# A three-layer block on one core: products with the high weights and products with the low weights, grouped by eight or taken in turns

## Chip, core and metric

The kernel runs on one core of one Trainium2 chip. The metric is the device time of one execution in microseconds. TensorE multiplies, ScalarE and VectorE evacuate, cast and subtract, SyncE issues the loads of the weights.

## What is computed

The input `x` is 256 tokens by 1024 features in float32. It goes through two mixer layers with an MLP each, and then through a layer with attention and a short convolution side by side:

```python
def first_block(x, ...):
    for l in range(2):
        h = rmsnorm(x, g[0])
        y = even_mixer(h, ...) if l % 2 == 0 else odd_mixer(h, ...)
        x = x + rmsnorm(y, g[1])
        h = rmsnorm(x, g[2])
        x = x + rmsnorm(sq_relu_mlp(h, mlp_w1[l], mlp_w2[l]), g[3])
    return x

def sq_relu_mlp(h, w1, w2):            # w1: 1024 x 4096, w2: 4096 x 1024
    return jnp.square(jax.nn.relu(h @ w1)) @ w2

def hybrid_layer(x, c, ...):
    h = rmsnorm_2(x, norm_g) * (1 + scale[:, None, :]) + shift[:, None, :]
    proj = h @ w_in                     # 1024 x 10240
    q, k, v, g_attn, cb, cc, cx, g_conv, m_attn, m_conv = jnp.split(proj, IN_OFFSETS, axis=-1)
    ...
    return x + gate[:, None, :] * (merged @ w_out)
```

The change concerns two kinds of these products: `h @ w1` of both MLPs, and the columns q, k, g_attn, cc, cx, cb and g_conv of `h @ w_in`.

## The kernel before

The weights come in units of 1 MB (a list `UNITS`, taken in order through a ring of buffers `raw`). Each unit is split into a high part `wh` (float32r, a cast on ScalarE) and a low part `wl` (the remainder, a subtraction on VectorE). The activation `h` is split likewise; for each slab `k` of 128 features, `hx[:, k, :, :]` holds the high part `hh` and the low part `hl` side by side, 256 tokens each. A product of float32 accuracy is high by high, plus high weights by low activation, plus low weights by high activation.

A feature-major unit ("F") holds 1024 input features by 256 output features. The 128 x 128 weights are the stationary operand, and the tokens stream. For most of these units both activation parts stream behind one load of the high weights: 512 columns into a whole bank of PSUM, `hh` into its first half and `hl` into its second. The low weights then take `hh` alone, 256 columns, and add to the bank's first half. The evacuation adds the two halves. In what follows a *wide* product is one of the 512-column ones with the high weights, a *narrow* product one of the 256-column ones with the low weights.

`both_parts(o, u, g)` issues this for one half `g` (128 output features) of a unit: 8 wide and 8 narrow products, one of each for every slab. It is called from `f_up` (roles `up0` and `up1`, 14 units each, the first two of the 16 up-projection units of a layer being token-major) and from `f_wide` (roles `aq`, `ak`, `ag`, `cc`, `cx`, `cb`, `cg`, 4 units each). The first `aq` unit is in `LOW_LAST`: it has a loop of its own, with all its wide products first, and isn't changed. The order of the work on TensorE is that of the loop over the units in the program. All waits of a group, for `hi`, `lo` and the bank, stand before its first product; the signal (`used`, `up_half`) goes with its last.

Down-projection units ("B") stream 512 weight columns behind `yh` or `yl`, in the order high, low, high; token-major units ("T") stream 512 weight columns behind `hh` or `hl`. Every product goes through one helper, `mm`, on line 672, so the trace has one line for all of them and they are told apart by their tiles. In the trace `hx,wh` is an F product with the high weights, `hx,wl` one with the low weights, `wh,hx` and `wl,hx` are T products, `yh` and `yl` stand for B products. LDWEIGHTS is the load of the stationary operand, on a row of its own, PEld.

Of the kernel before, what the change touches and what calls it, by code (L numbers as in the profile page):

```python
# [27 lines left out]
KT = D // P  # L28
# [240 lines left out]
def build(nc, a, out):  # L269
    ctx = ExitStack()  # L270
    with ctx:
# [284 lines left out]
        def slot(t, u):  # L556
            return part(t, u).rearrange("p (k c) -> p k c", k=SLABS[UNITS[u][0]])
# [112 lines left out]
        def _(eng):  # L670
            def mm(o, l, r, start, stop):
                return eng.matmul(o, l, r, start=start, stop=stop, skip_group_check=True)  # L672
# [65 lines left out]
            def both_parts(o, u, g):  # L738

                c = slice(g * P, (g + 1) * P)  # L740
                for k in range(KT):
                    mm(o[:, :], slot(wh, u)[:, k, c], hx[:, k, :, :].rearrange("p a t -> p (a t)"), k == 0, False)
                for k in range(KT):
                    m = mm(o[:, 0:SEQ], slot(wl, u)[:, k, c], hh[:, k, :], False, k == KT - 1)
                return m

            def f_up(u):
                layer, i = UPS.index(UNITS[u][4]), UNITS[u][5]
                for g in range(2):
                    n, o = up_block(u, g)  # L750
                    first = 2 * (i - 2) + g
                    if first < 2:
                        wait_evac(eng, at(UNITS[u][4].replace("up", "uw"), 1), first)
                    elif first == 2:
                        eng.wait_ge(S["x_row"], 2 * layer + 1)
                    else:
                        eng.wait_ge(S["up_sum"], n - 2)
                    both_parts(o, u, g).then_inc(S["used" if g else "up_half"], 1)

            def f_wide(u):  # L760

                n, w_hi, w_lo = WIDE_OF[u], slot(wh, u), slot(wl, u)
                if PAIR_OF[u] == (0, 1):
                    for t in range(TT):
                        wait_bank(eng, u, t)
                else:
                    for v in [v for v in WIDE_OF if v < u and PAIR_OF[v] == PAIR_OF[u]][-1:]:
                        wait_evac(eng, v)
                if u not in LOW_LAST:
                    for g in range(2):  # L770
                        m = both_parts(wide_bank(u, g), u, g)
                else:
                    for g in range(2):
                        for k in range(KT):
                            mm(wide_bank(u, g)[:, :], w_hi[:, k, g * P:(g + 1) * P], hx[:, k, :, :].rearrange("p a t -> p (a t)"), k == 0, False)
                    wait_low(eng, u)
                    for g in range(2):
                        for k in range(KT):
                            m = mm(wide_bank(u, g)[:, 0:SEQ], w_lo[:, k, g * P:(g + 1) * P], hh[:, k, :], False, k == KT - 1)
                m.then_inc(S["used"], 1)  # L780
# [1511 lines left out]
```

## Time and profile before

| | before |
|---|---|
| median of 3 runs | 974.04 us (973.6 to 974.58) |
| span of the profiled execution | 972.0 us |
| TensorE products busy | 964.2 us, 99%, 5192 of them |
| VectorE, ScalarE busy | 682.1 us (70%), 539.9 us (56%) |
| chain that ended last | TensorE 96%, line 672 alone 94% |
| granted TensorE clock | 0.999 of full speed over the span |

The profile gives no time of its own for the profiled execution beside its span; the span is 2.0 us below the median of the runs. A start in the timeline has a resolution of 0.01 us. The busy time of a row of products includes the latency of the last one, so paces are read from the starts and not from it.

### The profile page before, as it was taken

What the parts mean: (1) busy time and instruction counts of PE and PEld (TensorE: products, weight loads), DVE (VectorE), ACT (ScalarE), POOL (GpSimd) and SP (SyncE); (2) the same over time, 40 slices, a digit from 0 to 9 for tenths busy, and PEclk for the clock granted to TensorE, in tenths of its full rate; (3) what the DMA queues carried; (4) which work ended last, traced back from release to release, by engine and by line L of the source; (5) the groups of instructions that cost most, each with busy time, mean ns of one, the idle gap of its engine ahead of it and who ended that gap; (6) DMA issues with size and microseconds to landing.
All of it is one profiled execution on the core that took longest, in us unless ns stands there. A gap on an engine that the chain in (4) does not pass through costs nothing.

```text
span 972.0 us, 13041 instructions
## 1 busy us (share of the span) xinstructions
PE 964.2 (99%) x5192; PEld 832.9 (86%) x5192; DVE 682.1 (70%) x917; ACT 539.9 (56%) x733; POOL 13.9 (1%) x12
## 2 busy tenths in 40 slices
PE   9999999999999999999999999999999999999997
PEld 8898888888888888988888888887888888888886
DVE  6989646687677767866687767768554888756474
ACT  7844464664555457655674455558445576545533
POOL 0000000000000000000000000000000000002000
PEclk9999999999999999999999999999999999999999
DMA  9954526467776674534467777773855544566611
GB/s 330 302 174 130 173 89 197 130 228 265 226 242 225 231 245 135 178 130 130 152 216 256 242 225 243 247 219 117 271 194 178 170 139 165 173 215 221 207 51 43
DMA packets 122863, 187.27 MB, mean 193 GB/s; under 512 B 5331, under 2 KB 88756, under 8 KB 122804
## 3 DMA queue, kind: packets, MB, share of 16 engines
q1 hardware_dynamic: 122368, 186.05, 58.1%
q8 instruction: 41, 0.67, 0.3%
q10 hardware_dynamic: 436, 0.40, 0.1%
q14 instruction: 18, 0.15, 0.0%
HBM read 185.37 MB, written 1.06 MB: 192 GB/s over the span
## 4 chain that ended last, share of the span: by engine, by line
PE 96%; DVE 3%; ACT 1%; issue 0%; ACTq 0%
PE bank L672 94%; DVE arena L1236 1%; DVE wl L1230 1%; PE bank L936 1%; PE bank L1026 0%; ACT arena L1843 0%; DVE arena L1233 0%; DVE arena L1230 0%; PE bank L1109 0%; ACT L1843 0%; ACT wh L1848 0%; PE bank L879 0%; PE bank L735 0%; PE bank L945 0%; ACT sd L1843 0%
## 5 line engine op out<-in xcount | busy, mean ns | idle before, releaser
L1230 DVE TENSOR_TENSOR wl<-raw,wh 128x2048 fp32r<-128x2048 f32 (+1 forms) x157 | 356.7, 2275 | 152.1 <-ACT wh L1848 128.1
L1848 ACT CAST wh<-raw 128x2048 fp32r<-128x2048 f32 x155 | 294.7, 1911 | 142.7 <-PE bank L672 141.0
L672 PE MATMUL bank<-hx,wh 128*128 128x512 f32 (+1 forms) x1280 | 296.6, 364 | 0.1
L672 PEld LDWEIGHTS bank<-hx,wh 128*128 128x128 f32 x1280 | 219.4, 190 | 30.4 <-issue 0.7
L672 PE MATMUL bank<-wh,hx 128*128 128x512 f32 x576 | 184.5, 394 | 0.8 <-ACT hx L1843 0.5
L672 PE MATMUL bank<-hx,wl 128*128 128x256 f32 x1088 | 174.3, 282 | 0.0
L672 PEld LDWEIGHTS bank<-hx,wl 128*128 128x128 f32 x1088 | 156.7, 190 | 8.9
L672 PE MATMUL bank<-wh,yh 128*128 128x512 f32 (+1 forms) x420 | 163.4, 389 | 0.0
L672 PE MATMUL bank<-wl,yh 128*128 128x512 f32 (+1 forms) x420 | 162.7, 387 | 0.0
L672 PE MATMUL bank<-wh,yl 128*128 128x512 f32 (+1 forms) x420 | 162.6, 387 | 0.0
L672 PEld LDWEIGHTS bank<-wh,hx 128*128 128x128 f32 x576 | 107.8, 188 | 24.3 <-issue 2.0
L672 PE MATMUL bank<-wl,hx 128*128 128x512 f32 x288 | 112.2, 390 | 0.0
L672 PEld LDWEIGHTS bank<-wh,yl 128*128 128x128 f32 x420 | 78.9, 188 | 16.2
L672 PEld LDWEIGHTS bank<-wh,yh 128*128 128x128 f32 x420 | 78.9, 188 | 15.5
L672 PEld LDWEIGHTS bank<-wl,yh 128*128 128x128 f32 x420 | 79.0, 188 | 15.3
L1230 DVE TENSOR_TENSOR arena<-bank,arena 128x256 f32<-128x256 f32 (+1 forms) x89 | 40.7, 488 | 44.3 <-ACT arena L2195 29.5
L672 PEld LDWEIGHTS bank<-wl,hx 128*128 128x128 f32 x288 | 54.1, 188 | 10.6
L2195 ACT COPY arena<-bank 128x256 f32<-128x256 f32 x56 | 18.1, 376 | 74.1 <-PE bank L672 74.1
L1988 ACT COPY work<-bank 128x256 f32<-128x256 f32 x56 | 20.6, 368 | 52.2 <-PE bank L672 52.2
L1843 ACT ACTIVATE arena<-bank 128x512 f32<-128x512 f32 (+2 forms) x58 | 28.4, 498 | 32.9 <-PE bank L672 32.8
L1236 DVE SCALAR_TENSOR_TENSOR arena<-raw,cf,arena 128x256 f32<-128x256 f32 x84 | 40.7, 485 | 3.0
L1843 ACT ACT_TABLE_LOAD x26 | 33.4, 1283 | 4.3 <-PE bank L672 2.0
(187 smaller groups left out, 675.0 us busy)
## 6 DMA issues: line engine op xcount, KB each, us to landing
raw<-in_mlp_w SPq DMA_DIRECT2D x64, 1024.0 KB, 5.4
raw<-in_w_in SPq DMA_DIRECT2D x40, 1024.0 KB, 5.1
raw<-in_ev_w_in SPq DMA_DIRECT2D x19, 1024.0 KB, 5.5
raw<-in_w_ada SPq DMA_DIRECT2D x12, 1024.0 KB, 5.1
raw<-in_od_w_in SPq DMA_DIRECT2D x12, 1024.0 KB, 5.2
raw<-in_ev_w_out SPq DMA_DIRECT2D x6, 1024.0 KB, 4.9
raw<-in_od_w_out SPq DMA_DIRECT2D x4, 1024.0 KB, 4.8
raw<-in_w_o_conv SPq DMA_DIRECT2D x4, 1024.0 KB, 4.8
```

Source lines behind the costliest of these rows:

```text
L672: return eng.matmul(o, l, r, start=start, stop=stop, skip_group_check=True)
L936: m = eng.transpose(x_half(t, k), src[:, t, k * P:(k + 1) * P], ident[:, :])
L1230: return eng.tensor_tensor(o, x, y, op)
L1236: return eng.scalar_tensor_tensor(out=o, in0=x, scalar=c, in1=y, op0=op0, op1=op1)
L1843: return eng.activation(o, x, f, **more)
L1848: eng.copy(part(wh, u), part(raw, u)).then_inc(S["hi"], 1)
L1988: eng.copy(up_home(i)[:, g * SEQ:(g + 1) * SEQ], up_block(u, g)[1][:, SEQ:2 * SEQ]).then_inc(S["up_low"], 1)
L2195: m = eng.copy(wide_home(u, g), wide_bank(u, g)[:, SEQ:2 * SEQ])
```

## The change

The second loop header is taken out of `both_parts`. Before, the eight wide products of a half run one after another and then the eight narrow ones; after, each wide product is followed by the narrow one of the same slab. The products, their operands, the banks, the waits and the signals are the same.

```diff
             def both_parts(o, u, g):
 
                 c = slice(g * P, (g + 1) * P)
                 for k in range(KT):
                     mm(o[:, :], slot(wh, u)[:, k, c], hx[:, k, :, :].rearrange("p a t -> p (a t)"), k == 0, False)
-                for k in range(KT):
                     m = mm(o[:, 0:SEQ], slot(wl, u)[:, k, c], hh[:, k, :], False, k == KT - 1)
                 return m
```

TensorE's instruction order before, where the first `up0` unit follows on the token-major units of the same layer (the last columns name the bank that is written and the two operands; x8 is eight in a row):

```order
L672 MATMUL bank1<-wh_50,hx_53 128x512 x8
L672 MATMUL bank3<-ident_67,rs_77 128x128 x2
L672 MATMUL bank0<-hx_53,wh_50 128x512 x8
L672 MATMUL bank0<-hx_53,wl_51 128x256 x8
L672 MATMUL bank1<-hx_53,wh_50 128x512 x8
L672 MATMUL bank1<-hx_53,wl_51 128x256 x8
```

The same place after:

```order
L672 MATMUL bank1<-wh_50,hx_53 128x512 x8
L672 MATMUL bank3<-ident_67,rs_77 128x128 x2
L672 MATMUL bank0<-hx_53,wh_50 128x512
L672 MATMUL bank0<-hx_53,wl_51 128x256
L672 MATMUL bank0<-hx_53,wh_50 128x512
L672 MATMUL bank0<-hx_53,wl_51 128x256
```

The two rows of eight have become eight pairs; the rows ahead of them are where they were.

The second place is the end of the second `up0` unit, where the first down-projection unit of the MLP follows. Before:

```order
L672 MATMUL bank0<-hx_53,wh_50 128x512 x8
L672 MATMUL bank0<-hx_53,wl_51 128x256 x8
L672 MATMUL bank4<-wh_50,yh_54 128x512
L672 MATMUL bank4<-wl_51,yh_54 128x512
L672 MATMUL bank4<-wh_50,yl_55 128x512
```

After:

```order
L672 MATMUL bank0<-hx_53,wh_50 128x512
L672 MATMUL bank0<-hx_53,wl_51 128x256
L672 MATMUL bank0<-hx_53,wh_50 128x512
L672 MATMUL bank0<-hx_53,wl_51 128x256
L672 MATMUL bank4<-wh_50,yh_54 128x512
L672 MATMUL bank4<-wl_51,yh_54 128x512
L672 MATMUL bank4<-wh_50,yl_55 128x512
```

The group still ends with a narrow product, and the unit behind it is unchanged.

## Rows read from the trace of the kernel before

**Rows 1.** The page: span, busy times, chain that ended last, main DMA queue.
```profile
span 972.0 us, 13041 instructions
...
PE 964.2 (99%) x5192; PEld 832.9 (86%) x5192; DVE 682.1 (70%) x917; ACT 539.9 (56%) x733; POOL 13.9 (1%) x12
...
q1 hardware_dynamic: 122368, 186.05, 58.1%
...
PE 96%; DVE 3%; ACT 1%; issue 0%; ACTq 0%
PE bank L672 94%; DVE arena L1236 1%; DVE wl L1230 1%; PE bank L936 1%; PE bank L1026 0%; ACT arena L1843 0%; DVE arena L1233 0%; DVE arena L1230 0%; PE bank L1109 0%; ACT L1843 0%; ACT wh L1848 0%; PE bank L879 0%; PE bank L735 0%; PE bank L945 0%; ACT sd L1843 0%
```

**Rows 2.** TensorE's own waits: what waited for what, total, times, longest.
```profile
PE bank L672 <- DVE eps L1353: 0.9, 1, 0.9
PE bank L672 <- ACT hx L1843: 0.5, 1, 0.5
PE bank L672 <- ACT arena L1843: 0.3, 1, 0.3
```

**Rows 3.** Waits of all engines: the longest for TensorE.
```profile
ACT wh L1848 <- PE bank L672: 141.0, 50, 4.0
```

**Rows 4.** Busy time by stretches: length, engines, granted clock, DMA share, GB/s.
```profile
200.00:300.00 100.00, 100.00 (x527) 85.95 (x526) 77.43 (x99) 50.73 (x59) 0.00 (x0) 1.00 0.74 246
...
700.00:800.00 100.00, 100.00 (x565) 87.62 (x564) 66.38 (x101) 55.19 (x79) 1.30 (x1) 1.00 0.52 170
```

**Rows 5.** Timeline of TensorE, convolution units: start us, length us, what, count.
```profile
702.30 2.00 PE L672 MATMUL bank<-hx,wh 128*128 128x512 f32 x8
704.14 1.12 PE L672 MATMUL bank<-hx,wl 128*128 128x256 f32 x8
705.09 2.00 PE L672 MATMUL bank<-hx,wh 128*128 128x512 f32 x8
...
719.06 0.40 PE L672 MATMUL bank<-wh,hx 128*128 128x512 f32 x1
```

**Rows 6.** Timeline of TensorE: end of a long 512-column run and the group behind it.
```profile
722.03 0.39 PE L672 MATMUL bank<-wl,hx 128*128 128x512 f32 x1
...
729.51 0.39 PE L672 MATMUL bank<-wl,hx 128*128 128x512 f32 x1
...
729.97 1.98 PE L672 MATMUL bank<-hx,wh 128*128 128x512 f32 x8
731.78 1.12 PE L672 MATMUL bank<-hx,wl 128*128 128x256 f32 x8
732.73 2.00 PE L672 MATMUL bank<-hx,wh 128*128 128x512 f32 x8
```

**Rows 7.** Timeline of TensorE: first and last of a long 256-column run.
```profile
22.70 0.40 PE L672 MATMUL bank<-hx,wh 128*128 128x256 f32 x2
...
28.34 0.28 PE L672 MATMUL bank<-hx,wl 128*128 128x256 f32 x1
```

**Rows 8.** Timeline of TensorE: a run of 128-column products.
```profile
46.03 1.95 PE L672 MATMUL bank<-scr 128*128 128x128 f32 x16
```

**Rows 9.** Timeline of TensorE: 512-column products behind the last narrow group.
```profile
854.99 0.40 PE L672 MATMUL bank<-wh,yh 128*128 128x512 f32 x1
855.23 0.40 PE L672 MATMUL bank<-wl,yh 128*128 128x512 f32 x1
855.46 0.39 PE L672 MATMUL bank<-wh,yl 128*128 128x512 f32 x1
...
857.06 0.39 PE L672 MATMUL bank<-wh,yh 128*128 128x512 f32 x1
```

**Rows 10.** Groups of TensorE's products by shape: busy us, mean ns.
```profile
L672 PE MATMUL bank<-hx,wh 128*128 128x512 f32 x896 | 227.7, 396 | 0.0
```

**Rows 11.** Timeline of the weight loads in the convolution units.
```profile
703.92 1.13 PEld L672 LDWEIGHTS bank<-hx,wl 128*128 128x128 f32 x8
704.98 1.70 PEld L672 LDWEIGHTS bank<-hx,wh 128*128 128x128 f32 x8
```

## The prediction

> **What bounds the kernel now.** I read the profile from the outside in. The page comes first: its busy table and its chain of the work that ended last [rows 1]. TensorE is busy for 964.2 of 972.0 us, and 96% of the chain is TensorE, 94% on the one line L672 through which every product goes. The list of TensorE's own waits [rows 2] is three entries long and 1.7 us in all. So no other engine and no transfer sets the time; the other engines wait for TensorE (ScalarE's weight cast waits for it 141.0 us in total [rows 3]). What TensorE gains or loses in its own pace is the time, as long as nothing else comes up to it: VectorE is at 70%, ScalarE at 56% [rows 1], the main DMA queue at 58.1% of 16 engines [rows 1]. The granted clock is 1.00 in the stretches that hold the changed units [rows 4], which is the 2.4 GHz level, and TensorE has no idle time there before it could fall.
>
> A busy share of 99% says only that products follow one another. How dense they are must be read from their starts, so the next view is the timeline of TensorE in a stretch of convolution units [rows 5]. A group of eight 512-column and eight 256-column products repeats every 2.793 us: (719.06 - 702.30) / 6. This is 349.2 ns for each pair of one wide and one narrow product. The number beside each row, 2.00 us, is no pace: it includes the latency of the last product. Of the 2.793 us the wide eight take 1.84 us (702.30 to 704.14) and the narrow eight 0.95 us (704.14 to 705.09).
>
> **What the same products cost in long runs.** Nothing in this trace alternates the two widths product by product, so the pair's price must be bounded. Long runs of one width give the two bases:
>
> - 512 columns, many in a row: from 722.03 to 729.51 there are 33 starts (the low product, whose rows these are, comes every third time), 226.7 ns each [rows 6].
> - 256 columns, many in a row: from 22.70 to 28.34 there are 47 starts, 120.0 ns each [rows 7]. The low product comes every third time there, with the high ones between, so which weight tile is read does not matter.
>
> Eight pairs at these paces would be 8 x (226.7 + 120.0) = 2.773 us. The group takes 2.793. The 20 ns are the price of changing width, and one place tells where they lie. The group at 729.97 is the only one that follows directly on a run of 512-column products of the same kind: its wide eight take 1.81 us and the group 2.76 us (729.97 to 732.73), against the 2.793 of the usual group [rows 5, 6]. So what costs is coming from a narrow product into a wide one, about 28 ns per group, and going from wide to narrow gives about 7 ns back (2.766 measured against 2.773 at the two paces).
>
> The rise lasts longer than one product. After the last narrow group of the convolution, at 854.99, the next wide starts are 240 and 230 ns apart [rows 9], and from 854.99 to 857.06 there are 9 spacings in 2.07 us, where the steady pace gives 2.04. So some 30 ns are lost over up to nine products, and the first one bears about a quarter to a third of them (240 - 227 at a resolution of 10 ns; I use 7, what a narrow product after a wide one gives back).
>
> **The change, term by term.** `both_parts` is called for 2 halves of 28 up-projection units and 27 of the 28 convolution and attention units (the unit listed in `LOW_LAST` keeps its own loop), so 110 groups of eight pairs, 880 pairs. The counts agree: 896 wide products are 880 plus the 16 of that unit [rows 10]. Nothing is added or removed: the same 1760 products, weight loads, banks and signals. All waits (for high and low weights, for the bank) stand ahead of the first product before and after, and both halves of a bank are finished by the same last product, so evacuations, casts and loads are released as before. These edits cost nothing. What changes is that each group has 8 entries into a wide product where it had 1.
>
> - Weight load under its cover. A load starts when the product before it starts, and the loads of the wide products run at the pace of the products above them: the first load of the wide eight stands at 704.98, with the last narrow product, and its own product at 705.09 [rows 5, 11]. Runs of 128-column products, which are shorter than a load, go at about 112 ns per start (16 in 1.95 us; less the 0.27 us that one takes, over 15) [rows 8]. So a load is done within a 120 ns narrow slot and within a 227 ns wide one. Exposed load time: 0 now, so no large gain is to be had by covering it, and none is lost as each wide product's load now lies under one narrow product.
> - The narrow product, always right after a wide one: 120.0 less the 7 ns of the first of a run = 113 ns.
> - The wide product, always right after a narrow one: 226.7 plus the first step of the rise, about 7 = 233 to 234 ns.
> - Pair: 113 + 233.5 = 346.5 ns against 349.2 now: -2.7 ns. Times 880 = -2.4 us. I take -2.2 us, the same as the two paces alone (346.7), because the two 7 ns terms look like one piece of work that moves from the narrow product to the wide one behind it.
>
> Sum: 974.04 - 2.2 = 971.8 us. The page's span is 972.0 us; the 2.0 us between it and the median of 974.04 lie outside the trace and stay. Later engines have room: ScalarE and VectorE would run 0.2% tighter.
>
> The bounds of the pair: below, both products at their best (226.7 + 113 = 340 ns), -8.1 us. Above, a wide product at the worst place of the rise, between 227 and 240 at the resolution of [rows 9], 236 taken, and a narrow one that gives nothing back, 120: 356 ns, +6.0 us. The extreme, the whole 20 ns net in every pair, is 366.7 ns, +15.4 us; it needs a transient of several products to be paid in one product, so it only gives weight to the upper side.
>
> The Trainium skill, "TensorE: Matmul & The Clock Gate", section "LDWEIGHTS (loading the stationary operand)", gives a load as columns / 1.2 GHz, an estimate of 107 ns for 128; by that, the trace agrees roughly (112 ns).
>
> **The rivals.**
>
> 1. *Order makes no difference.* Costs belong to each product whatever stands beside it, so the pair stays at its present average, 230 + 119 = 349 ns, and the time at 974.0 us. For it: all 880 products keep their width, and the price of a change of width seen so far is 2.5 ns of a 349 ns pair (20 over eight). Against it: the group at 729.97 is 27 ns shorter only by what came before it. The skill has this rule on the same page, section "Back-to-back issue gap": the isolated spacing is N / 2.4 + 2.5 ns whatever comes next. By it a pair would be an estimated 325 ns in either order; the trace shows 349, so its size is off, and the order is what this rival leaves open.
> 2. *The rise restarts at every wide product and never settles* (the slower side). The pace of a wide run needs several products to come down to 226.7 after a narrow one [rows 9]; with a narrow one in between each time it never does. If a wide product then costs 233 to 236 and the narrow one 119 to 120, a pair is 352 to 356 ns: +2.5 to +6.0 us, 976.5 to 980.0. It decides against the change from 351.4 ns per pair on (0.2% of the time over 880 pairs). For it: eight entries for one, with a transient of known size. Against: the first product after an entry has only a part of it, and the narrow one gives as much back.
> 3. *Both at their best.* The narrow product after each wide one leaves its surroundings as in a wide run: 340 ns per pair, -8.1 us, 965.9 us. For it: only that both numbers occur. Against: the wide product behind a narrow run is slower, at 854.99 as in the groups of [rows 5] (1.84 us for eight, against 1.81 in [rows 6]).
> 4. *The change does not do what it says* has no chance worth a number: the instruction order shows the alternation at all 110 groups.
>
> **How the numbers follow.** My forecast (346 to 348 ns) 0.36, rival 1 (348 to 350.5) 0.28, rival 2 0.26, rival 3 or something between it and the forecast 0.10. A measurement of this kernel tells about 0.2%, 1.95 us, from no change. The forecast's 2.2 us lies just beyond this bound, so I give two thirds of its chance to faster, the rest to same. Faster: 0.24 + 0.10 + a little = 0.37. Same: 0.12 + 0.24 = 0.36. Slower: 0.27. The likeliest case alone would be 970.5 to 972.8. The range over all goes from the middle of rival 3 (968.5) to the upper part of rival 2 (979.5).
>
> **What would show it.** In the timeline of the changed kernel a group should take 16 starts in about 2.77 us, each wide start followed by the narrow one 233 ns later and this by the next wide one 113 ns later. TensorE's waits stay under 2 us, the counts of section 5's groups stay, the span falls by some 2 us, all of it inside the 110 groups; runs of 512-column products outside them keep 226.7 ns. The prediction is wrong if a wide product takes 236 ns or more, or a narrow one 119 or 120 though a wide one precedes it, or if TensorE begins to wait for another engine.

## The result, and the profile after

The changed kernel takes 976.21 us (median of 16 runs, 975.64 to 977.5); the kernel before takes 973.82 us beside it (16 runs, 973.53 to 974.8). The ratio is 1.0022, 95% interval 1.0015 to 1.0028: slower by 2.1 us, between 1.5 and 2.7; the plain difference of the two medians, 2.4 us, lies in the same interval. I had forecast 971.8 us. The time is inside my range of 968.5 to 979.5, but on the other side of the kernel before: the kernel got slower where I had said faster. It is the direction of my second rival, at or just under the lower end of its +2.5 to +6.0 us.

The page of the changed kernel, with the lines that answer to [rows 1]:

```profile
span 973.7 us, 13041 instructions
...
PE 965.6 (99%) x5192; PEld 830.7 (85%) x5192; DVE 682.5 (70%) x917; ACT 539.8 (55%) x733; POOL 13.9 (1%) x12
...
PE 92%; DVE 3%; ACT 2%; DMA 2%; issue 1%; SPq 0%; DVEq 0%; ACTq 0%
```

The span has grown by 1.7 us, and the counts are the same. TensorE's share of the chain that ended last is 92% where it was 96%. That comes from the first 37 us, ahead of all changed products, where the chain now goes through two loads of weights and their casts; from there on it is TensorE as before. TensorE's own waits, to be set against [rows 2]:

```profile
PE bank L672 <- DVE eps L1352: 0.9, 1, 0.9
PE bank L672 <- ACT hx L1842: 0.5, 1, 0.5
PE bank L672 <- ACT arena L1842: 0.2, 1, 0.2
```

They total 1.6 us, against 1.7 before. So no new wait was made: TensorE waits for nobody and yet is slower, and the loss must lie in its own pace. The granted clock is still 1.00 in the same two stretches as in [rows 4]:

```profile
200.00:300.00 100.00, 100.00 (x522) 85.34 (x521) 77.24 (x99) 50.36 (x58) 0.00 (x0) 1.00 0.74 246
700.00:800.00 100.00, 100.00 (x563) 86.64 (x562) 65.19 (x100) 53.88 (x79) 1.30 (x1) 1.00 0.52 174
```

Next the starts. This is the timeline of TensorE over the first full stretch of up-projection groups: 32 pairs between a 1-column product and the down-projection.

```profile
220.42 0.50 PE L672 MATMUL bank<-ones,arena 128*128 128x1 f32 x4
220.78 0.49 PE L672 MATMUL bank<-hx,wh 128*128 128x512 f32 x1
221.10 0.28 PE L672 MATMUL bank<-hx,wl 128*128 128x256 f32 x1
221.22 0.40 PE L672 MATMUL bank<-hx,wh 128*128 128x512 f32 x1
221.45 0.28 PE L672 MATMUL bank<-hx,wl 128*128 128x256 f32 x1
221.57 0.40 PE L672 MATMUL bank<-hx,wh 128*128 128x512 f32 x1
...
231.82 0.40 PE L672 MATMUL bank<-hx,wh 128*128 128x512 f32 x1
...
232.17 0.40 PE L672 MATMUL bank<-wh,yh 128*128 128x512 f32 x1
```

From 221.22 to 231.82 there are 30 pairs: 10.60 us, 353.3 ns per pair. The whole stretch takes 232.17 - 220.78 = 11.39 us. The kernel before took 11.28 us for it, by the same two places of its timeline:

```profile
221.12 0.49 PE L672 MATMUL bank<-hx,wh 128*128 128x512 f32 x1
...
232.40 0.40 PE L672 MATMUL bank<-wh,yh 128*128 128x512 f32 x1
```

And this is the last stretch of convolution groups in the same trace, 32 pairs behind a 128-column product:

```profile
845.50 0.47 PE L672 MATMUL bank<-hx,wh 128*128 128x512 f32 x1
845.82 0.27 PE L672 MATMUL bank<-hx,wl 128*128 128x256 f32 x1
845.93 0.40 PE L672 MATMUL bank<-hx,wh 128*128 128x512 f32 x1
...
856.33 0.40 PE L672 MATMUL bank<-hx,wh 128*128 128x512 f32 x1
...
856.68 0.39 PE L672 MATMUL bank<-wh,yh 128*128 128x512 f32 x1
```

From 845.93 to 856.33 there are again 30 pairs, of the same products in the same order: 10.40 us, 346.7 ns per pair. This is to the tenth the pace that my forecast stands on.

So the same alternation runs at two paces. Taken from the single starts of the trace (ns), the slow one repeats every three pairs, the fast one every two:

| pace | starts, wide then narrow, ns | sum |
|---|---|---|
| slow | 241, 120, 236, 113, 233, 117 | 1060 per 3 pairs = 353.3 |
| fast | 233, 117, 231, 112 | 693 per 2 pairs = 346.7 |

The first few products of a stretch differ, then the pattern holds for as long as nothing foreign comes between. I went through all 32 stretches, which hold the 110 changed groups: 21 of them (86 groups) run in the slow pattern, 11 (24 groups) in the fast one. All 12 stretches behind a 1-column product, with 48 groups, are slow. Summed from the first product of each stretch to the first foreign product behind it, the stretches take 2.10 us more than before: 1.41 in the up-projection, 0.69 in the convolution and attention units. That is the whole of the measured 2.1 us.

In this one pair of profiles the span grew by only 1.7 us. The other 0.4 us stand ahead of the change: the first changed product starts 0.36 us earlier than before, at 197.35 (after) against 197.71 (before):

```profile
197.35 0.48 PE L672 MATMUL bank<-hx,wh 128*128 128x512 f32 x1
...
197.71 0.48 PE L672 MATMUL bank<-hx,wh 128*128 128x512 f32 x1
```

One more thing stands in the single starts. Which pace a stretch of the changed kernel takes goes with the spacing behind its very first wide product. Where a 128-column product stands ahead, this spacing is 312 to 314 ns in all seven stretches at 346.7 ns per pair and 316 in all three at 353.3. Where a 256-column product stands ahead, it is 417 ns in the four stretches at 346.7 and 419 or 420 in the four at 353.3. So 2 or 3 ns at the way in go together with 6.6 ns in every pair behind it. This is read from one kernel; in a later one (the lead of one in all units) 314 ns stands ahead of a slow stretch as well as a fast one.

**Is it the weight load?** The rows of the loads look the same at both paces. The load of the wide product's weights starts 2 to 3 ns after the narrow product above it and its row lasts 187 or 188 ns, in a slow stretch (225.34) as in a fast one (850.32):

```profile
225.34 0.28 PE L672 MATMUL bank<-hx,wl 128*128 128x256 f32 x1
225.34 0.19 PEld L672 LDWEIGHTS bank<-hx,wh 128*128 128x128 f32 x1
...
850.32 0.28 PE L672 MATMUL bank<-hx,wl 128*128 128x256 f32 x1
850.33 0.19 PEld L672 LDWEIGHTS bank<-hx,wh 128*128 128x128 f32 x1
```

The row of a load is longer than the 120 ns at which narrow products follow one another, so it is no measure of what a load takes from the engine. When the array is free for the next load is not in the trace.

### The profile page after: what moved, and what is told of

It is laid out like the page before. It is cut to its first block, busy times and chain, and to the rows that moved or that the text cites. A ratio compares the mean times of both kernels' runs of the same rounds, so it can differ in the third digit from the quotient of the medians.

```text
span 973.7 us, 13041 instructions
## 1 busy us (share of the span) xinstructions
PE 965.6 (99%) x5192; PEld 830.7 (85%) x5192; DVE 682.5 (70%) x917; ACT 539.8 (55%) x733; POOL 13.9 (1%) x12
## 4 chain that ended last, share of the span: by engine, by line
PE 92%; DVE 3%; ACT 2%; DMA 2%; issue 1%; SPq 0%; DVEq 0%; ACTq 0%
PE bank L672 90%; DMA raw<-in_ev_w_in 2%; DVE wl L1229 1%; DVE arena L1235 1%; ACT wh L1847 1%; PE bank L935 1%; ACT arena L1842 1%; PE bank L1025 0%; DVE arena L1232 0%; ACT L1842 0%; DVE arena L1229 0%; PE bank L1108 0%; PE bank L735 0%; PE bank L878 0%; DVE hx L1235 0%
## 5 line engine op out<-in xcount | busy, mean ns | idle before, releaser
L672 PE MATMUL bank<-hx,wh 128*128 128x512 f32 (+1 forms) x1280 | 387.2, 367 | 0.1
L672 PE MATMUL bank<-hx,wl 128*128 128x256 f32 x1088 | 298.1, 281 | 0.0
L672 PEld LDWEIGHTS bank<-hx,wh 128*128 128x128 f32 x1280 | 226.1, 189 | 40.9 <-issue 0.7
L672 PEld LDWEIGHTS bank<-hx,wl 128*128 128x128 f32 x1088 | 202.8, 189 | 0.3
```

## The experiments

Two theories stand against each other. **A** is my rival 2 as I had reasoned it: each entry from a narrow into a wide product has its price. **B** came from the table above: the starts settle into a repeating pattern, and the way in decides which. All variants keep the 880 wide and 880 narrow products, unless it is said otherwise. In the code cuts `hx[...]` stands for the whole moving operand of a wide product. Each ratio is to the kernel before, run beside the variant (medians 974.14 to 974.31 us).

**Other orders of the same sixteen products.** The first, second and fourth kernel replace the loop in `both_parts` by a given order (W wide, N narrow):

```diff
-                for k in range(KT):
-                    mm(o[:, :], slot(wh, u)[:, k, c], hx[...], k == 0, False)
-                    m = mm(o[:, 0:SEQ], slot(wl, u)[:, k, c], hh[:, k, :], False, k == KT - 1)
+                wide = low = 0
+                for p in "WWNN" * 4:      # runs of four: "WWWWNNNN" * 2; skewed: "W" + "WN" * 7 + "N"
+                    if p == "W":
+                        mm(o[:, :], slot(wh, u)[:, wide, c], hx[...], wide == 0, False)
+                        wide += 1
+                    else:
+                        m = mm(o[:, 0:SEQ], slot(wl, u)[:, low, c], hh[:, low, :], False, low == KT - 1)
+                        low += 1
```

Runs of two. Expected:

> Runs of two: two wide products, two narrow ones, four times per group. Theory A (price per change of width: every entry from narrow into wide costs a part of the 28 ns rise, cut off when the run ends): half as many entries as in the changed kernel, two wide starts at 233 and 236 ns and two narrow at 113 and 119 make 701 ns per two pairs, 350.5 ns per pair against 349.2 before and 351 on average after; time about 975 us, between the two kernels (ratio 1.001 to 1.002). Theory B (the starts settle into a repeating pattern, and which one is decided by how a group is entered; the number of changes of width by itself says nothing): the pace of a group repeats exactly within a stretch, is 346.7 in some stretches and higher in others, and the time need not lie between the two kernels.

Measured: 973.93 us, ratio to the kernel before 0.9997 (0.9988 to 1.0006). Not between the two kernels, as A has it, but at the time of the kernel before. The timeline, behind a 1-column product:

```profile
560.87 0.63 PE L672 MATMUL bank<-hx,wh 128*128 128x512 f32 x2
561.33 0.40 PE L672 MATMUL bank<-hx,wl 128*128 128x256 f32 x2
...
563.65 0.62 PE L672 MATMUL bank<-hx,wh 128*128 128x512 f32 x2
```

Four periods take 2.78 to 2.79 us; a group takes 2.787 us, though it has four entries into wide products where the kernel before has one and takes 2.793.

Runs of four. Expected:

> Runs of four: four wide, four narrow, twice per group. Theory A: two entries per group, wide 233 + 236 + 228 + 233, narrow 113 + 119 + 120 + 120, 1402 ns per four pairs, 350.5 ns per pair, +1.2 us over the kernel before (about 975 us). Theory B: no order between runs of 1, 2, 4 and 8 follows; each has a repeating pattern of its own.

Measured: 975.05 us, ratio 1.0009 (1.0000 to 1.0018). A's number, 975 us, is met here. But A had put the runs of two and of four at the same 350.5 ns per pair, and they differ: with half the entries of the runs of two, the runs of four are slower, 2.807 us per group by the starts behind a 1-column product against 2.787. A's prices, each read at a single border, do not give that.

Runs of sixteen: both halves' wide products, then both halves' narrow ones.

```diff
 # f_up
-                    both_parts(o, u, g).then_inc(S["used" if g else "up_half"], 1)
+                    wide_half(o, u, g)
+                for g in range(2):
+                    low_half(outs[g], u, g).then_inc(S["used" if g else "up_half"], 1)
 # f_wide
-                    for g in range(2):
-                        m = both_parts(wide_bank(u, g), u, g)
+                    for g in range(2):
+                        wide_half(wide_bank(u, g), u, g)
+                    for g in range(2):
+                        m = low_half(wide_bank(u, g), u, g)
```

> Runs of sixteen: both halves' wide products first, then both halves' narrow ones, so one entry into wide per unit instead of two. Theory A: 55 entries less at 20 ns net, -1.1 us against the kernel before, ratio 0.9989, if the later end of the first half makes no evacuation late. Theory B: the same here, since every run is long enough to settle. If the evacuation of the up-projection becomes late, TensorE shows waits of its own for ScalarE or VectorE on the bank, and the time is over that of the kernel before.

Measured: 973.23 us, ratio 0.9993 (0.9984 to 1.0002). The interval takes in no change and the -1.1 us of the expectation. In the timeline, one up-projection unit:

```profile
565.63 3.82 PE L672 MATMUL bank<-hx,wh 128*128 128x512 f32 x16
569.28 2.08 PE L672 MATMUL bank<-hx,wl 128*128 128x256 f32 x16
571.20 0.40 PE L672 MATMUL bank<-wh,yh 128*128 128x512 f32 x1
```

A unit takes 5.57 us against 2 x 2.793 = 5.586, 20 ns less, as forecast from one entry fewer. TensorE's waits are 1.7 us as before, so the later end of the first half costs nothing.

The skewed alternation. Expected:

> Alternation as in the changed kernel, but the wide products run one ahead: wide, (wide, narrow) seven times, narrow. The inner order is the same and the group borders are narrow, narrow, wide, wide, so there is one change of width less per group. Theory A: 7 entries instead of 8, time within 0.3 us of the changed kernel or a little under it. Theory B: the entries of the groups differ from those of the changed kernel, so other groups land in the 346.7 ns pattern and others in the 353.3 ns one; the time can move by up to 5 us to either side, and single groups should show one of these two paces, or a third, and nothing between.

Measured: 975.90 us, ratio 1.0017 (1.0008 to 1.0026), at the changed kernel's time within the intervals. A had forecast this time, so it doesn't decide. More telling is its first stretch of four groups:

```profile
221.08 0.72 PE L672 MATMUL bank<-hx,wh 128*128 128x512 f32 x2
221.63 0.28 PE L672 MATMUL bank<-hx,wl 128*128 128x256 f32 x1
221.75 0.39 PE L672 MATMUL bank<-hx,wh 128*128 128x512 f32 x1
...
223.49 0.39 PE L672 MATMUL bank<-hx,wh 128*128 128x512 f32 x1
223.72 0.40 PE L672 MATMUL bank<-hx,wl 128*128 128x256 f32 x2
```

From 221.75 to 223.49 there are five pairs in 1.74 us, 348 ns at this resolution; by the single starts they are 230 and 117 ns, or 346.7 per pair. Behind the same 1-column product the changed kernel falls into the slow pattern. The next group, which comes in over the border narrow, narrow, wide, wide, takes 2.815 us and comes to the slow starts (241, 120, 236) after its first few products. This gave the test further below.

**Is it the bank, or the weight buffer?** In the convolution and attention units, each narrow product adds to the other bank than the wide one ahead of it:

```diff
-                    for g in range(2):
-                        m = both_parts(wide_bank(u, g), u, g)
+                    for k, g in [(k, g) for k in range(KT) for g in range(2)] + [(KT, 0)]:
+                        if k < KT:
+                            mm(wide_bank(u, g)[:, :], w_hi[:, k, g * P:(g + 1) * P], hx[...], k == 0, False)
+                        if (k, g) != (0, 0):
+                            kl, gl = (k, 0) if g else (k - 1, 1)
+                            m = mm(wide_bank(u, gl)[:, 0:SEQ], w_lo[:, kl, gl * P:(gl + 1) * P], hh[:, kl, :], False, kl == KT - 1)
```

> As the changed kernel, but in the 27 convolution and attention units the two halves are interleaved, so that each narrow product adds to the other bank than the wide product ahead of it. Theory B (pattern of starts by width): the bank is no part of it; in the convolution stretch the pair costs 346.7 or 353.3 ns, as in the changed kernel, and nothing else. Theory C (the narrow product, or the wide one behind it, waits for the sums that its neighbour is still adding to the same bank): the waits go, and the pairs of the convolution stretch come down to 346.7 ns or less everywhere, about 3 us faster than the changed kernel.

Measured: 977.02 us, ratio 1.0026 (1.0017 to 1.0036). Theory C, a wait for sums in the same bank, falls: nothing came down, and inside each unit the pairs still show 353.3 (such as 241, 120, 236, 113, 233, 117) or 346.7 ns. The edit changes the way in too: each unit now begins with two wide products and ends with two narrow ones. After that 21 of the 27 units are slow and 6 fast, where in the changed kernel 17 were slow and 10 fast.

Widths grouped by eight as before, but the weight tiles taken in turns:

```diff
-                    mm(o[:, :], slot(wh, u)[:, k, c], hx[...], k == 0, False)
-                    m = mm(o[:, 0:SEQ], slot(wl, u)[:, k, c], hh[:, k, :], False, k == KT - 1)
+                for k in range(KT):
+                    mm(o[:, :], slot((wh, wl)[k % 2], u)[:, k, c], hx[...], k == 0, False)
+                for k in range(KT):
+                    m = mm(o[:, 0:SEQ], slot((wl, wh)[k % 2], u)[:, k, c], hh[:, k, :], False, k == KT - 1)
```

> Widths grouped by eight as in the kernel before, but the weight tiles take turns within each run (high, low, high, ... for the wide ones; low, high, ... for the narrow ones). The products of the odd slabs so compute something else; widths, counts and sizes are those of before. Theory B (only widths count): 2.793 us per group, time as before, ratio 1.000. Theory D (it is the turn from one weight buffer to the other, not the width, that costs): the time is at or over that of the changed kernel, ratio 1.002.

Measured: 974.30 us, ratio 1.0001 (0.9992 to 1.0010). Theory D falls too: seven turns from one weight buffer to the other in each run of eight cost nothing. The kernel leaves out high weights by low activation on the odd slabs, so it serves for its time alone. The timeline shows the group of [rows 5] again. The last wide product of a run and the first narrow one read the same tile here, so they share a row, at 701.98; the next such row stands at 704.77, 2.79 us later:

```profile
701.98 0.50 PE L672 MATMUL bank<-hx,wl 128*128 128x512 f32 x2
702.32 0.28 PE L672 MATMUL bank<-hx,wh 128*128 128x256 f32 x1
...
704.77 0.50 PE L672 MATMUL bank<-hx,wl 128*128 128x512 f32 x2
705.11 0.28 PE L672 MATMUL bank<-hx,wh 128*128 128x256 f32 x1
```

What is left is the order of the widths.

**The change in the up-projection alone.** The convolution and attention units keep two loops.

```diff
+                    if UNITS[u][4] in UPS:
                         m = mm(o[:, 0:SEQ], slot(wl, u)[:, k, c], hh[:, k, :], False, k == KT - 1)
+                if UNITS[u][4] not in UPS:
+                    for k in range(KT):
+                        m = mm(o[:, 0:SEQ], slot(wl, u)[:, k, c], hh[:, k, :], False, k == KT - 1)
```

> The change in the 28 up-projection units alone. In the trace of the changed kernel 12 of the 14 stretches of up-projection groups that follow a 1-column or 128-column product run in the 353.3 ns pattern. So the up-projection should carry nearly its share by count or more: 56 groups, +33 ns for those in the slow pattern, less some 10 ns at each entry behind a foreign product: +1.3 to +1.6 us, ratio 1.0014. If the two kinds of units act on each other in some other way, the part is not what the trace of the changed kernel gives for these groups.

Measured: 975.56 us, ratio 1.0016 (1.0007 to 1.0025). The up-projection carries 1.4 us by the trace, and its groups run as they do in the changed kernel, while those of the other units take their time of before: the two kinds of units don't act on each other. (The expectation counts 14 stretches, by pairs of units. In the trace there are 16, and 14 of them are slow: the 12 behind a 1-column product and 2 of the 4 behind a 128-column one.)

**Many orders in one kernel.** Each stretch of up-projection groups has an order of its own.

> One look, not for its time: each of the 14 stretches of up-projection groups has another order of its 8 wide and 8 narrow products, and the four rounds of convolution units have four of them. Read from the trace, per order: the time of the second to fourth group of a stretch. Theory A (price per change of width, cut off by the run's length): the group's time rises with the number of entries into wide products. Theory B: no such order; the group time minus 8 x 346.7 ns scatters between 0 and 55 ns, whatever the number of entries, and is the same at every repetition of a stretch. The best orders of this look are candidates for a kernel that beats both.

This kernel ran once (974.37 us) and is read for its starts alone: second to fourth group of each stretch behind a 1-column product (ns), with 2773 as eight pairs at 346.7:

| order of a group | entries into wide | group |
|---|---|---|
| WWWWWWWWNNNNNNNN (before) | 1 | 2793, 2793, 2794 |
| WWWWWNNNNNWWWNNN | 2 | 2794, 2793, 2793 |
| WWWWWWWNNNNNNNWN | 2 | 2806, 2807, 2807 |
| WWWNNNWWWNNNWWNN | 3 | 2797, 2796, 2797 |
| WWNNWWNNWWNNWWNN | 4 | 2787, 2787, 2786 |
| WNNWWNNWWNNWWNNW | 4 | 2786, 2787, 2787 |
| WWWNNWNNWWWNNWNN | 4 | 2800, 2800, 2800 |
| WWNWNNWWNWNNWWNN | 5 | 2801, 2790, 2803 |
| WNWNWWNNWNWNWWNN | 6 | 2813, 2813, 2814 |
| WNWNWNWWNNWNWNWN | 7 | 2794, 2800, 2793 |

The rows of two of these stretches, of 32 pairs each, from the first product behind the 1-column ones to the down-projection: seven and one in a row, 559.61 to 570.92, 11.31 us; runs of two, 604.81 to 616.05, 11.24 us.

```profile
559.25 0.50 PE L672 MATMUL bank<-ones,arena 128*128 128x1 f32 x4
...
570.92 0.40 PE L672 MATMUL bank<-wh,yh 128*128 128x512 f32 x1
...
604.45 0.50 PE L672 MATMUL bank<-ones,arena 128*128 128x1 f32 x4
...
616.05 0.40 PE L672 MATMUL bank<-wh,yh 128*128 128x512 f32 x1
```

The time does not rise with the number of entries: four can be quicker than one, and two slower than seven. Theory A falls as a law; what it says is borne out between runs of eight and of sixteen alone. The spread, 13 to 41 ns over 2773, is within B's 0 to 55 (two more orders with six entries, not in the table, take 2813 or 2814), and most values repeat from group to group; those of two orders do not within the three groups. Two orders stood in two stretches each behind 128-column products, and both show two times for their second group: strict alternation 2774 and 2837 ns, six wide, six narrow, two wide, two narrow 2780 and 2802. So the two paces are no special case of the strict alternation.

**Change the way in.** The decisive pair of kernels issues the narrow product one (or two) wide products late, and lets it stay owed across the borders of groups and of the two units of a stretch:

```diff
+            owed = []
+
+            def pay(rest):
+                while len(owed) > rest:
+                    o, u, g, k, done = owed.pop(0)
+                    m = mm(o[:, 0:SEQ], slot(wl, u)[:, k, g * P:(g + 1) * P], hh[:, k, :], False, k == KT - 1)
+                    if done is not None:
+                        m.then_inc(S[done], 1)
+
+            def ahead(o, u, g, done):
+                c = slice(g * P, (g + 1) * P)
+                for k in range(KT):
+                    mm(o[:, :], slot(wh, u)[:, k, c], hx[...], k == 0, False)
+                    owed.append((o, u, g, k, done if k == KT - 1 else None))
+                    pay(1)                         # a lead of two: pay(2)
 # f_up, in place of both_parts; the end of a stretch pays what is owed
-                    both_parts(o, u, g).then_inc(S["used" if g else "up_half"], 1)
+                    ahead(o, u, g, "used" if g else "up_half")
+                if UNITS[u][5] % 2 or UNITS[u][5] == 2:
+                    pay(0)
```

Lead of one, up-projection alone. Expected:

> The change in the up-projection units alone, as in the run with the up-projection alone (ratio 1.0016), and with as many turns from wide to narrow inside a stretch; but each stretch of up-projection groups begins with two wide products, and one narrow product stays owed across the borders of its groups and is issued behind the next wide one. So only the entry of a stretch differs, and its last two products are narrow. The skewed kernel showed 347 ns pairs in the first group of such a stretch. Theory B (the entry decides which pattern a stretch falls into): the stretches behind a 1-column product go from 353.3 to 346.7 ns per pair, 48 groups at about 50 ns less, so about 2.5 us less than with the up-projection alone: ratio to the kernel before 0.999, range 0.998 to 1.0. Theory A (every entry into a wide product has its price): no change against the run with the up-projection alone, 1.0016.

Measured: 973.62 us, ratio 0.9991 (0.9982 to 1.0000), against 1.0016 for the up-projection alone without the lead. The same stretch as at the top:

```profile
220.64 0.50 PE L672 MATMUL bank<-ones,arena 128*128 128x1 f32 x4
221.00 0.72 PE L672 MATMUL bank<-hx,wh 128*128 128x512 f32 x2
221.56 0.28 PE L672 MATMUL bank<-hx,wl 128*128 128x256 f32 x1
221.68 0.39 PE L672 MATMUL bank<-hx,wh 128*128 128x512 f32 x1
...
231.73 0.39 PE L672 MATMUL bank<-hx,wh 128*128 128x512 f32 x1
231.96 0.40 PE L672 MATMUL bank<-hx,wl 128*128 128x256 f32 x2
232.20 0.40 PE L672 MATMUL bank<-wh,yh 128*128 128x512 f32 x1
```

From 221.68 to 231.73 there are 29 pairs in 10.05 us, 346.6 ns each, where the changed kernel has 353.3; the stretch takes 11.20 us against 11.39 and 11.28. All 12 stretches behind a 1-column product do the same. The alternation is as dense as in the changed kernel; in the order of widths only the second product and the last of a stretch are others. By the single starts these pairs are 230 and 117 ns each, so there are two sequences at the fast pace, this one and the 233, 117, 231, 112 of the table.

One thing goes with the lead: a narrow product no longer reads the slab of the wide one ahead of it. That can't be what sets the pace. In the changed kernel every narrow product reads the same slab as the wide one ahead, and 11 stretches are fast and 21 slow; with a lead of one in all units (below) none does inside a stretch, and again some are fast and some slow.

Lead of two. Expected:

> As the first run of this call (up-projection alone, owed across groups), but with a lead of two: a stretch begins with three wide products and ends with three narrow ones; between them the order is the same alternation. Theory B: another entry, so again one of the known paces, 346.7 or 353.3 ns per pair, for a whole stretch, with nothing between; which one is open. Theory A: as with a lead of one, within 0.1 us per stretch.

Measured: 973.74 us, ratio 0.9993 (0.9985 to 1.0002). All 12 stretches are at 346.7 ns, none between the two paces:

```profile
221.20 0.96 PE L672 MATMUL bank<-hx,wh 128*128 128x512 f32 x3
222.00 0.28 PE L672 MATMUL bank<-hx,wl 128*128 128x256 f32 x1
222.12 0.39 PE L672 MATMUL bank<-hx,wh 128*128 128x512 f32 x1
...
231.82 0.39 PE L672 MATMUL bank<-hx,wh 128*128 128x512 f32 x1
```

Here 222.12 to 231.82 holds 28 pairs in 9.70 us, 346.4 ns each at this resolution.

Lead of one in the convolution and attention units as well:

> The same order in the convolution and attention units too; owed narrow products are issued before any foreign product. Theory B: the up-projection's groups at 2.773 us as in the run before this one; in the convolution and attention units each stretch takes one of the patterns, and which one cannot be said beforehand: between 971.8 (all at 346.7) and 975.5 us (all at 353.3). Theory A: at or over the changed kernel, ratio 1.002.

Measured: 974.69 us, ratio 1.0002 (0.9994 to 1.0011). The up-projection stays fast; of the 16 other stretches 12 are slow and 4 fast, against 7 and 9 in the changed kernel. The same lead that helps behind a 1-column product does not help elsewhere, and mostly hurts: which pattern it is belongs to the whole entry, not to the lead. TensorE's own waits total 2.8 us in this profile, the most of all variants.

The candidate: the lead in the up-projection, runs of sixteen in the other units.

> The candidate to beat both: owed order in the up-projection, and in the convolution and attention units both halves' wide products first and then both halves' narrow ones (2.783 us per group by the trace of the kernel with runs of sixteen). Theory B: 56 groups at 20 ns less and 54 at 10 ns less than before, and some 10 ns less at each entry behind a foreign product: -1.9 us, ratio 0.998. Theory A: +1.0 us, ratio 1.001.

Measured: 972.71 us, ratio 0.9985 (0.9976 to 0.9993). It beats both kernels, by 1.5 us (0.7 to 2.3) against the one before, which is 0.15%.

**The books.** For each kernel, the 32 stretches summed from the starts of its profile, less those of the kernel before, beside the measured ratio. 974 us is 1.

| kernel | stretches, us | as a ratio | measured |
|---|---|---|---|
| changed | +2.10 | 1.0022 | 1.0022 |
| runs of two | -0.68 | 0.9993 | 0.9997 |
| runs of four | +0.88 | 1.0009 | 1.0009 |
| runs of sixteen | -0.70 | 0.9993 | 0.9993 |
| skewed | +1.52 | 1.0016 | 1.0017 |
| other bank | +2.51 | 1.0026 | 1.0026 |
| weight tiles in turns | +0.03 | 1.0000 | 1.0001 |
| up-projection alone | +1.44 | 1.0015 | 1.0016 |
| lead of one, up-projection | -0.92 | 0.9991 | 0.9991 |
| lead of two, up-projection | -0.79 | 0.9992 | 0.9993 |
| lead of one, all | +0.49 | 1.0005 | 1.0002 |
| candidate | -1.36 | 0.9986 | 0.9985 |

All are within their intervals. The pace of the changed products alone accounts for every one of these times.

## Why the prediction was wrong, by its own steps

**What bounds the kernel** was right. TensorE's pace is the time; the waits stay at 1.6 to 1.7 us in the changed kernel and the candidate, and the clock stays at 1.00. That the move of instructions costs nothing by itself, and that weight loads stay covered, was right as far as the runs show: the fast pair is the sum of the two settled paces, 226.7 + 120.0, so nothing of a load shows in it, and the rows of the loads are the same in the slow stretches. That no part of the slow pair's 6.6 ns is a load stays likely, not shown.

**"Pair: 113 + 233.5 = 346.5 ns"** is the step that failed. As a number it is true in 11 stretches of 32, to the tenth. As a statement about all 880 pairs it is false: 86 of 110 groups run at 353.3 ns. The two terms in it, "120.0 less the 7 ns of the first of a run = 113 ns" and "the first step of the rise, about 7", were read at, or estimated for, places where a long run of the other width lay ahead. I used each as the price of a product that depends on its one neighbour. It does not: in the slow pattern a narrow product behind a wide one takes 113, 117 and 120 ns in turn, and a wide one behind a narrow one 233, 236 and 241. The mean over the changed kernel's pairs is 235 and 117 ns. The 7 ns themselves were of the right size where I read them: by the single starts the first wide product behind the narrow run of [rows 9] takes 233 ns. My reason for them was loose, as 240 - 227 would be over 40% of the 30 ns and not a quarter to a third. And the second one there takes 236, more than the first, which a price of the single border has no place for.

**The bounds** held: 353.3 lies in my 340 to 356 ns. A single wide product took up to 241 ns, every third one of the slow pattern, over the 236 that I had as the upper bound of one. With it came the signs that I had set for being wrong: a wide product of 236 ns or more, and a narrow one of 120 behind a wide one.

**Rival 2** named the right sign and very nearly the size, "352 to 356 ns", and something of the ground: a wide product behind a narrow one does not come down to 226.7. Its "+2.5 to +6.0 us" has all 880 pairs slow; a fifth of the groups (24 of 110) fell into the fast pattern, and 2.1 us was left. Nothing in the trace of before told how many would, so that the time came out as near to no change as it did is chance as far as my working goes. It was wrong in that it made a price per entry: runs of two have half the entries of the changed kernel and four times those of the kernel before, and come out level with the latter. Nor does the rise start anew at each wide product: the starts settle into a repeating pattern, at a pace that depends on the way in. I gave it 0.26 and the forecast 0.36. The trace of before had the warning in it. At 854.99 the loss went on over several products, so the pace had a memory longer than one product [rows 9], and a sum of pair prices read at single borders could not stand for a sequence that has a border at every product.

**Rival 1**, that order makes no difference, falls: the same 1760 products gave 972.71 to 977.02 us by their order alone. The Trainium skill ("TensorE: Matmul & The Clock Gate", section "Back-to-back issue gap") gives the spacing of isolated products by a formula in N alone; "whatever comes next" was my reading of it. Taken so it does not hold for this stream, where every product has a load: one and the same 512-column product started the next after 231 or 241 ns.

**Rival 3** falls as well: no stretch came to 340 ns per pair.

## What to carry to other kernels

When TensorE is the bound and never waits, a few ns per product remain, and they depend on the sequence of widths, with a memory of several products. Don't sum them from prices read at single borders: try the order on the chip, and read the starts over whole stretches, because the same order can run at two paces. Long runs of one width were the safe choice here (a group took 2.793 us in runs of eight and 2.783 in runs of sixteen, in nearly every place past the first group of a stretch); a strict alternation can be quicker (346.7 against 349.2 ns here), but only if its entry falls right, and moving one product at the start of a stretch is enough to change that. Which entry is right had to be tried: no rule for it came out of these runs.

## What the runs showed of the hardware that I had not expected

A stream of 512- and 256-column products with a weight load each does not have one spacing per width. It runs into a repeating pattern, and strict alternation has two paces that hold over a stretch: 1060 ns per 3 pairs, and 693 ns per 2. The fast pace is the sum of the two settled ones, 226.7 + 120.0 = 346.7; the slow one is 6.67 ns more. All three are multiples of 6.67 ns (34, 18 and, for the slow pair, 53 of them), and it looks as if starts were held to a step of this size, with a rest carried on to the next products. But that is an observation on three numbers, and one order of the table above, at 2796.7 ns per group, fits only half this step. It is not shown. What in the chip makes the step, why the 1-column entry leads to one pattern and some of the 128- and 256-column ones to the other, and whether a pattern can be foretold for an order that hasn't been run, stays open; no run here looks inside.
